# Second attention layer of a two-layer decoder: index scores ahead of the latents, five query projections moved under the top-k rounds, the others made five head pairs early

## The reference

```
q, c_kv, q_idx, k_idx, w_idx, qc = split(rmsnorm(x) @ w_in)      # 1024 | 256 | 8*64 | 64 | 8 | 256 columns
c_kv  = rmsnorm(c_kv)                                            # the latent, 256 wide
s     = relu(q_idx . k_idx / 8)                                  # 8 index heads
score = sum_h w_idx[h] * s[h] / sqrt(8), masked to causal keys
idx   = top_k(score, 64)                                         # keys each query may see
attention over these keys, 16 heads of 64: keys c_kv @ w_uk, values c_kv @ w_uv, plus relative bias
cross attention of 4 heads over 256 memory tokens with queries qc
x     = x + concat(attention, cross) @ w_out
```

## Time and profile before

| | |
|---|---|
| three runs | 1554.76, 1555.86, 1561.9 us; median 1555.86 |
| profiled execution, first to last instruction (its own time; no other is recorded for it) | 1555.8 us |
| busy in it | PE 1525.7, DVE 1326.4, ACT 1131.3, POOL 90.4 us |
| stretch the change touches | 431.4 (first index product) to 572.4 us (residual) |
| mean granted TensorE clock | 0.995 |

### The profile page before, as it was taken

How to read it: one execution, slowest core, us unless ns; L and a number is a source line. 1 busy time by engine, 2 the same in 40 slices (tenths; PEclk the granted TensorE clock), 3 DMA queues, 4 the chain that set the end, 5 groups by cost and what they waited for, 6 DMA issues and landing times.

```text
span 1555.8 us, 25342 instructions
## 1 busy us (share of the span) xinstructions
PE 1525.7 (98%) x8159; PEld 1287.2 (83%) x8159; DVE 1326.4 (85%) x1806; ACT 1131.3 (73%) x1507; POOL 90.4 (6%) x68
## 2 busy tenths in 40 slices
PE   9999999999999999999999999999999999999997
PEld 8999967888887778888888888888888888888886
DVE  6888858777758778998998998998998998998997
ACT  6565556445547668788788788878888878878875
POOL 2422100000010000000000000000000000000000
PEclk9999999999999999999999999999999999999999
DMA  9944536666513477999999999999999999999993
GB/s 290 227 135 137 162 103 194 186 181 194 155 49 82 156 282 283 409 392 370 380 396 362 378 398 359 389 394 354 392 391 353 395 390 353 398 387 350 401 385 116
DMA packets 227061, 455.38 MB, mean 293 GB/s; under 512 B 12912, under 2 KB 120576, under 8 KB 227008
## 3 DMA queue, kind: packets, MB, share of 16 engines
q1 hardware_dynamic: 222800, 439.52, 78.4%
q0 software_dynamic: 4208, 15.22, 3.8%
HBM read 445.52 MB, written 9.18 MB: 292 GB/s over the span
## 4 chain that ended last, share of the span: by engine, by line
PE 91%; DVE 4%; ACT 3%; issue 1%; DMA 0%; SPq 0%; ACTq 0%; DVEq 0%
PE ps L740 26%; PE ps L742 26%; PE ps L741 26%; PE ps L991 5%; PE ps L993 2%; PE ps L1153 2%; PE ps L830 1%; PE ps L860 1%; ACT w_hi L1191 1%; DVE w_lo L1543 1%; DVE small L1632 1%; PE ps L845 1%; DVE z L1610 1%; DVE z L1629 1%; PE ps L1095 0%
## 5 line engine op out<-in xcount | busy, mean ns | idle before, releaser
L1543 DVE TENSOR_TENSOR w_lo<-big,w_hi 128x1024 fp32r<-128x1024 f32 x837 | 983.6, 1213 | 135.5 <-ACT w_hi L1191 59.6
L1456 ACT CAST w_hi<-big 128x1024 fp32r<-128x1024 f32 x672 | 693.6, 1056 | 139.5 <-PE ps L742 136.5
L740 PE MATMUL ps<-w_hi,m_hi 128*128 128x512 f32 (+1 forms) x1008 | 391.9, 389 | 1.4 <-ACT qT L1248 1.3
L741 PE MATMUL ps<-w_lo,m_hi 128*128 128x512 f32 (+1 forms) x1008 | 389.2, 386 | 0.0
L742 PE MATMUL ps<-w_hi,m_lo 128*128 128x512 f32 (+1 forms) x1008 | 389.2, 386 | 0.0
L740 PEld LDWEIGHTS ps<-w_hi,m_hi 128*128 128x128 f32 x1008 | 189.5, 188 | 41.4 <-issue 2.2
L742 PEld LDWEIGHTS ps<-w_hi,m_lo 128*128 128x128 f32 x1008 | 189.5, 188 | 38.4
L741 PEld LDWEIGHTS ps<-w_lo,m_hi 128*128 128x128 f32 x1008 | 189.6, 188 | 37.2
L1191 ACT CAST w_hi<-big 128x1024 fp32r<-128x1024 f32 (+1 forms) x171 | 166.0, 982 | 42.1 <-PE ps L742 36.7
L740 PE MATMUL ps<-w_hi,h_two 128*128 128x512 f32 (+1 forms) x464 | 182.6, 394 | 0.0
L742 PE MATMUL ps<-w_hi,h_two 128*128 128x512 f32 (+1 forms) x464 | 179.8, 387 | 0.0
(11 more groups left out here) (270 smaller groups left out, 1580.9 us busy)
## 6 DMA issues: line engine op xcount, KB each, us to landing
big<-in_odd_w_gate SPq DMA_DIRECT2D x112, 1024.0 KB, 7.3
big<-in_odd_w_up SPq DMA_DIRECT2D x112, 1024.0 KB, 7.4
big<-in_odd_w_down SPq DMA_DIRECT2D x112, 1024.0 KB, 7.4
big<-in_even_w_in SPq DMA_DIRECT2D x42, 512.0 KB, 4.6
big<-in_even_w_gate SPq DMA_DIRECT2D x22, 512.0 KB, 4.5
big<-in_even_w_up SPq DMA_DIRECT2D x22, 512.0 KB, 3.9
big<-in_even_w_down SPq DMA_DIRECT2D x22, 512.0 KB, 4.6
big<-in_w_out SPq DMA_DIRECT2D x20, 512.0 KB, 3.6
```

What stands on the lines that cost most here:

```text
L740: mm(dst, a[0], b[0], start=start, stop=False, **kw)
L741: mm(dst, a[0], b[1], start=False, stop=False, **kw)
L1456: nc.scalar.copy(w_hi[:, slot, :], ring[s][:, (u % 2) * UNIT:(u % 2 + 1) * UNIT]).then_inc(s_hi, 1)
L1543: return V.tensor_tensor(dst, src, lead.bitcast(F32), ALU.subtract)
```

## The change

The order of the index stage is now: weights (8 columns, with the norm transposes), key, two query units, scores of index heads 0 and 1, third query unit, heads 2 and 3, fourth, heads 4 to 7. Four PSUM banks instead of two hold the scores. Then the latents. Then the new list `PROJ` sets the order of all projections: queries 0 to 2 (the latent turned behind query 1, without the 16 idle matmuls), keys 0 and values 0, scores of pair 0, queries 3 and 4, all ahead of step 0. Step g projects keys and values g+1 and, for g = 0 to 4, query g+5. Queries 6 to 9 live in tiles that the index stage has left. GpSimd makes the low parts of the first ten units. `steps` is unrolled for this layer.

```diff
+MADE_IN = {0: 5, 1: 6, 2: 7, 3: 8, 4: 9}
+PROJ = [("q", 0), ("q", 1), ("q", 2), ("k", 0), ("v", 0), ("q", 3), ("q", 4)]
+for _g in range(PAIRS - 1):
+    PROJ += [("k", _g + 1), ("v", _g + 1)] + ([("q", MADE_IN[_g])] if _g in MADE_IN else [])
+POOL_SPLITS = PROJ[:PROJ_AT["q", MADE_IN[0]] + 1]
+def step_projections(g):
+    return [key for key in (("k", g + 1), ("v", g + 1), ("q", MADE_IN.get(g))) if key in PROJ_AT]
...
-           (1, 6, 0): 1, (1, 6, 1): 1, (1, 6, 5): 1, (1, 7, 0): 1, (1, 7, 1): 1, (1, 7, 5): 2,
+           (1, 6, 5): 1, (1, 7, 0): 1, (1, 7, 1): 1, (1, 7, 5): 2,
...
 # GpSimd
-            for g in range(2):
-                for m in range(3):
+            for key in POOL_SPLITS:
+                u, n = proj_unit(key)
...
 # PE: index stage
+            idx_queries(0)
+            idx_queries(1)
+            idx_scores(0)
+            idx_queries(2)
+            idx_scores(1)
+            idx_queries(3)
+            idx_scores(2)
+            idx_scores(3)
...
             def turn_latent():
-                keep_warm(8, 4)
                 pe.wait_ge(s_cch, 4)
...
-                keep_warm(8, 4)
 # PE: step
                     if not now.cross:
-                        project(nxt, 0)
+                        if l == 0:
+                            project(nxt, 0)
                         turn_values(now)
-                        project(aft, 0)
+                        if l == 0:
+                            project(aft, 0)
...
+                if l == 1:
+                    turn_values(now)
+                    for key in step_projections(now.g):
+                        if key[0] == "q":
+                            scores(nxt)
+                        project_odd(key)
+                    if now.g not in MADE_IN:
+                        scores(nxt)
+                    turn_probs(now, 0)
+                    turn_probs(now, 1)
+                    mix(now)
+                    return
...
+                for n, key in enumerate(PROJ[:PROJ_AT["k", 1]]):
+                    project_odd(key)
+                    if key == ("q", 1):
+                        turn_latent()
+                    if key == ("v", 0):
+                        pe.wait_ge(s_rl, IDX_HEADS)
+                        scores(pair_at(1, 0))
 # ACT: step
-                if now.l == 1:
-                    hi_mat(aft, 0)
                 exps(now, 0)
...
+                elif now.kind == "odd":
+                    made = step_projections(now.g)
+                    if now.g == 0:
+                        evac_odd(("q", 4))
+                    for key in made[:1]:
+                        evac_odd(key)
+                    values()
+                    exps(now, 1)
+                    for key in made[1:2]:
+                        evac_odd(key)
+                    probsT(now, 0)
+                    for key in made[2:]:
+                        evac_odd(key)
+                    outs(hi, now, 0)
+                    probsT(now, 1)
+                    outs(hi, now, 1)
+                    for key in step_projections(now.g + 1):
+                        hi_odd(key)
+                    outs(hi, now, 2)
...
 # ACT: ahead of step 0
+            evac_odd(("q", 2))
+            evac_odd(("k", 0))
+            hi_odd(("k", 1))
+            evac_odd(("v", 0))
+            hi_odd(("v", 1))
+            evac_odd(("q", 3))
+            hi_odd(("q", 5))
...
 # DVE: step
-                    lo_mat(aft, 0)
                     outs(lo_now, now, 1)
-                    lo_mat(aft, 1)
-                    lo_mat(aft, 2)
+                    if now.kind == "odd":
+                        for key in step_projections(now.g + 1):
+                            lo_odd(key)
                     outs(lo_now, now, 2)
                 if nxt is not None and not now.cross:
                     head_scores(nxt)
 # DVE: meanwhile, in the top-k rounds
-                if k == 0:
-                    split_by_pool(pair_at(1, 0), 0, 1, 2)
-                if k == 4:
+                if k == 2:
                     dve.wait_ge(s_cch, 1)
...
-                if k == 5:
-                    split_by_pool(pair_at(1, 1), 0)
+                if k == 3:
                     dve.wait_ge(s_cch, 3)
```

More of the change, by code:

```diff
@@ L165, in __init__, with add @@
         self.slot, self.previous, self.loads, self.at = [], [], [], {}
+        self.pool, self.nth = [], []
         last, loaded = [None] * SLOTS, [0] * SLOTS
-        def add(key, slot, loads=1):
+        def add(key, slot, loads=1, pool=False):
             self.at[key] = len(self.slot)
@@ L246, in pair_at, with steps @@
     return Pair(l, g // 2, g % 2)
-def steps(l, engine, one):
+def steps(engine, one):
     last = PAIRS // 2 - 3
@@ L504, in width, with query, proj_unit, idx_bank @@
         def width(pair, m):
-            return RC * P if pair.kind == "odd" and m > 0 else UNIT
+            return UNIT
+        def query(pair):
+            g = pair.g
+            if g < 2 * NBR:
+                return qT[:, g % 2, g // 2, :]
+            return (zq[:, 512:768], zq[:, 768:1024], kiT, qT[:, 0, 0, :])[g - 2 * NBR]
+        def proj_unit(key):
+            return U.at[("proj", *key)], RC * P if key[0] != "q" else UNIT
+        def idx_bank(h):
+            return ps[:, (0, 1, 5, 6)[h % 4], 0:CAUSAL]
+        def split_done(units):
+            return s_plo if U.pool[units[0]] else s_lo
         def ring_slot(i):
@@ L558, in stream_loads @@
                         load(0, 0, [U.at[key]], w_o[l][:, key[2]:key[2] + 1, :])
+            def stream_loads():
+                span = range(1, PAIRS // 2)
+                load_pair(pair_at(0, 0))
+                load_pair(pair_at(0, 1))
+                with sp.Fori(1, PAIRS // 2) as i:
+                    for par in range(2):
+                        load_pair(Pair(0, i, par, span))
+                late_loads(0)
             def mem_load(n):
@@ L744, in split @@
             def split(i, first, units, c, n=UNIT):
-                pe.wait_ge(s_lo, along(i, first, [u + 1 for u in units]))
+                pe.wait_ge(split_done(units), along(i, first, [U.nth[u] for u in units]))
                 slot = U.slot[units[0]]
@@ L1248, in evac, with evac_odd, hi_odd @@
                 nc.scalar.copy(dst, ps[:, pair.bank(m), 0:SEQ]).then_inc(S["evacuated"], 1)
+            def evac_odd(key):
+                S = s_at[1]
+                what, g = key
+                u, _ = proj_unit(key)
+                n = PROJ_AT[key]
+                act.wait_ge(s_used, u + 1)
+                if what == "q":
+                    if g == NPAIR - 1:
+                        act.wait_ge(S["scores"], 2)
+                    dst = query(pair_at(1, g))
+                elif what == "k":
+                    if g >= 2:
+                        act.wait_ge(S["scores"], 2 * (g - 2) + 2)
+                    dst = kT[:, g % 2, :]
+                else:
+                    if g >= 1:
+                        act.wait_ge(S["turned_v"], g)
+                    dst = vT[:, :]
+                nc.scalar.copy(dst, ps[:, 3 + n % 2, 0:SEQ]).then_inc(S["evacuated"], 1)
+            def hi_odd(key):
+                u, n = proj_unit(key)
+                hi(0, 0, [u], n)
             def exps(pair, hh):
@@ L1324, in stream @@
                     evac(a, m)
-                    if l == 0:
-                        hi_mat(b, m)
-                steps(l, act, step)
+                    hi_mat(b, m)
+                steps(act, step)
             def ebuf_copy():
```

309 lines of the change are left out of this document (168 added, 141 removed).

## The result

The change makes the kernel slower: 1580.66 us (median of 4 runs, 1579.72 to 1583.01) against 1556.8 us (4 runs), a ratio of 1.0148, 95% interval 1.0135 to 1.0162. The profiled execution took 1577.9 us from first to last instruction, against 1555.8 us: 22.1 us more. Its mean granted clock is 0.989, before 0.995.

What follows compares the result with a forecast made beforehand. TensorE and VectorE are both nearly full, so the order of their waits decides. 1555.8 + 13.4 (4.2 + 10.1 - 2.7 + 1.8) + 8 for the clock = 1577 us; range 1562 to 1585.

Steps and rivals of the forecast that it cites:

- rival A: The forecast itself: longer circle of waits per step, clock falling in most waits; 1570 to 1585 us, chance 0.57.
- The circle: Steps 1 to 3: waits from one pair's first score read to the next; 11.3 us instead of 7.94, +10.1 us.
- Step 0: First step, ending at 486.6 instead of 482.44 us, with the table load taken as exposed: +4.2 us.
- Steps 4 to 6: Late steps with less query work: 9.5, 7.5 and 5.4 us, together 22.4 against 25.1: -2.7 us.
- The clock: TensorE's clock falls in four waits of 3.4 us, 6 us in all; about 2 more elsewhere: +8 us.
- The upper bound of 1.7: Most that each of four TensorE waits could lose to the slower clock: 1.7 us, with 1.5 taken.
- VectorE's wait: In each step, a wait of 3.6 us ahead of the keys' low part, 0.6 more ahead of the query's.
- The index stage: Reordered scores ahead of top-k: two more heads of ReLU and sum, first max near 456.8 us, 2.8 sooner.
- z(0): Moment at which VectorE reads the first scores of pair 0: near 471.0 us, 3.6 us sooner.
- Tail: From pair 7's first score read to the residual: 4.9 us of query products go, waits replace them: +1.8 us.
- broken stretches: Clock loss in steps 5 and 6 and 3 us idle before pair 7's probabilities: about 2 us, 0 to 4.
- Rival D: Faster, 1549 us, if VectorE's wait ahead of its small low parts stays at 0.55 us or below; chance 0.07.

## Why the prediction was right

It gave 1577 us and a range of 1562 to 1585, and slower with 0.84; the median is 1580.66. Its rival A, a longer circle with the clock falling in most waits, is what happened. Point by point:

- **The circle, right.** 11.3 us were added up, 11.40 to 11.42 measured with the clock up. Of its surplus the order's share is 2.1 us (9.28), and cast and low part's 1.4 for 1.41 left out. After each wait stands what the prediction named: 3.22 us on TensorE for the copy of the keys (forecast 3.4).
- **Step 0, right.** 15.6 forecast, 15.82 measured, the table load exposed at 475.22 us between the cast of query 5 and the first exponential.
- **Steps 4 to 6, right.** 9.5, 7.5 and 5.4 at an unchanged clock; 9.69, 7.56 and 5.34.
- **The clock, right in kind.** Four waits at 1.5 us were forecast for 6 us in all; three of the four cost 2.84, 2.56 and 1.50 and the fourth nothing, 6.9. The upper bound of 1.7, from one stretch of the first layer, was no bound: from 490 to 496.5 us the scores and nearly the whole query run at the half clock. By the Trainium skill, page TensorE: Matmul & The Clock Gate, section HAM oscillation, every wait would be paid; this trace shows three in four.
- **VectorE's wait, right where the clock stayed up.** 3.6 forecast ahead of the keys' low part; 3.58 measured in step 3, 6.42 and 6.16 in steps 1 and 2, where the clock fell. 0.49 ahead of the query's (forecast 0.6).
- **The index stage, the step that failed.** "Two more heads of ReLU and sum" were to follow the last scores. There are four: the scores of heads 4 to 7 are issued together at 450.89 us, and VectorE's eight pieces (four heads) take 3.84 us from 452.37 (timelines of TensorE and VectorE):

```profile
450.89 1.58 PE L1120 MATMUL ps<-zq 64*128 64x128 f32 x16
...
452.37 3.84 DVE L1972 SCALAR_TENSOR_TENSOR pr<-z,small,pr 128x128 f32<-128x128 f32 x8 [2.31 <-ACT z L1553]
```

  Beside GpSimd's small pass the first piece of the causal mask then takes 0.77 us instead of 0.29. The first max was expected 25.4 us after the start of the stage and came after 27.33, before 28.20. So the new order gains 0.9 us there and 2.1 at z(0), not 2.8 and 3.6. In absolute times this is hidden (457.38 and 471.12, near the forecast 456.8 and 471.0), since this execution began the stage 1.4 us sooner.
- **Tail, near in sum, mixed in cause.** +1.8 was forecast at an unchanged clock, +2.2 measured, but with the clock down. Windows and timeline of TensorE in the changed kernel, then both in the kernel before (L781 and L740 start output unit 0, L899 and L845 come behind its last matmul):

```profile
550.00:552.00 2.00, 0.85 (x5) 0.31 (x3) 1.90 (x7) 1.18 (x3) 0.00 (x0) 0.78 0.87 326
552.00:562.00 10.00, 6.85 (x23) 4.61 (x24) 6.24 (x16) 4.77 (x13) 0.00 (x0) 0.53 0.40 145
...
558.22 0.77 PE L781 MATMUL ps<-w_hi,m_hi 128*128 128x512 f32 x1 [0.65 <-DVE w_lo L1694]
...
562.52 0.49 PE L899 MATMUL ps<-con,pr 128*128 128x128 f32 x3
```

```profile
531.36:572.44 41.08, 39.09 (x218) 31.18 (x217) 29.78 (x64) 24.76 (x52) 0.00 (x0) 1.00 0.64 223
...
538.18 0.50 PE L740 MATMUL ps<-w_hi,m_hi 128*128 128x512 f32 x1 [1.32 <-ACT qT L1248]
...
541.04 0.49 PE L845 MATMUL ps<-con,pr 128*128 128x128 f32 x3
```

  Output unit 0, 12 matmuls in both, takes 4.30 us instead of 2.86. These 1.4 us are the clock's, and are what came of the 2 us forecast for broken stretches and the idle time before pair 7's probabilities; steps 5 and 6 lost nothing (7.57 and 5.34, with idle matmuls 7.56 and 5.34). So an estimate for the tail at an unchanged clock is +0.8. The run with the old step order shows that taking queries 8 and 9 out of the tail bought nothing: 42.58 us, with waits in place of the products and again the half clock in output unit 0.
- **The sum, right in part by luck.** The rows give 6.9 + 1.4 = 8.3 us for the clock, where 8 were forecast, and 22.9 - 8.3 = 14.6 us for the rest, where 13.4 were. Inside the rest the index stage missed by 1.5 us one way and the tail by about 1.0 the other. That these cancel is luck.
- **Rival D's point of decision** was the wait of 0.55 us. With the old step order the steps are those of before, and steps 5 and 6 are 1.8 us shorter together; it ends at 1561, not at 1549, because step 0 (+2.4) and the tail (+1.5) give back more.

One thing stays open: why the clock held after the wait of step 3, equal in length to its neighbours. In the run with keys copied first, waits of 2.56 us brought it down in steps 1 and 2 and not in steps 3 and 4.

## What to carry to other kernels

In a loop of several engines that each have a fixed order, write down the circle of waits from one step's event to the next's, with each cast and copy in it, before moving a step: here one large unit cast at the end instead of the start, and one product put ahead of the turned probabilities, made steps of 7.9 us 3.5 us longer, though no engine got more work. Work moved into an earlier stage helps only if that stage has a gap on the same engine. And a wait that a new order opens on TensorE costs a second time where the clock falls in it; a few idle matmuls measure that part, and take it away where they stand.

## What the runs showed of the hardware

- GpSimd's pass over SBUF held up VectorE's two-input operation in SBUF until it ended: 2.75 us for 0.56 beside a pass of 2.36. It held up a one-input operation between SBUF tiles too (L2012, 1.97 us for 0.36). The max and match_replace rounds beside passes of 2.40 us kept their times (0.62, and 0.28 and 0.41 us).
- In the run with the keys copied first the clock went from 1.00 to 0.50 around waits of 2.56 us in two of four steps. What decides between them is not shown.
- The start of the same unchanged stretch differs by up to 3.8 us between profiled executions, more than some of the terms that were to be read: differences belong between events of one execution.
